# A shorter router, expert weights loaded further ahead, and a spread-out convolution in a two-block transformer kernel

## The reference, cut to what matters

```python
h = rmsnorm(x, norm1_g); proj = h @ w_in
ya = windowed_gqa(...)                      # 8 heads, window of 128
ym = mlstm_branch(qm, km, vm, om, gates...) # first: a depthwise convolution of 5 taps over q and k, then silu
u  = gates[:, :D] * (ya @ w_branch_attn) + gates[:, D:] * (ym @ w_branch_mlstm)
x  = x + u @ w_out
x  = x + hier_moe(rmsnorm(x, norm2_g))
# hier_moe: 4 groups of 8 experts; argmax group; top 2 experts in it, softmax weights
# each expert: (silu(t @ w_gate[e]) * (t @ w_up[e])) @ w_down[e], 1024 -> 512 -> 1024
```

## Time and profile before

| what | value |
|---|---|
| median of 3 runs | 2285.16 us (2284.2 to 2285.91) |
| the profiled execution: its time | 2284.88 us |
| the profiled execution: its span | 2283.0 us |
| mean granted clock of PE | 0.955 |
| PE busy | 2037.0 us, 89% of the span |
| DVE, ACT, POOL busy | 672.9, 590.4, 678.4 us |
| DMA traffic | 362.43 MB, of which the 192 expert loads are 201 MB |

### The profile page before, as it was taken

The page is one execution under the profiler, slowest core; times in us unless marked ns, Lnnn a source line. Parts: engine busy times, 40 slices in busy tenths (PEclk is TensorE's granted clock), DMA queues, the critical chain, the costliest instruction groups (busy, mean ns, idle before and its releaser), DMA issues.

```text
span 2283.0 us, 29374 instructions
## 1 busy us (share of the span) xinstructions
PE 2037.0 (89%) x10746; PEld 1446.5 (63%) x10747; DVE 672.9 (29%) x1145; ACT 590.4 (26%) x987; POOL 678.4 (30%) x383
## 2 busy tenths in 40 slices
PE   8987899999999999999999989997893887778884
PEld 7864688888888878888887756775782322222221
DVE  2348631110052243111007685124546000000002
ACT  2126333332212222333221325444420000000000
POOL 4421134444514434444451522222230000000000
PEclk9998999999999999999999989999896899999997
DMA  7311023332313324333231311210116899999996
GB/s 213 108 56 39 19 93 101 94 99 93 130 54 95 105 77 121 101 92 101 92 129 45 117 56 56 65 56 19 55 62 242 342 426 427 427 426 426 425 423 242
DMA packets 155405, 362.43 MB, mean 159 GB/s; under 512 B 16671, under 2 KB 88991, under 8 KB 130752
## 3 DMA queue, kind: packets, MB, share of 16 engines
q1 hardware_dynamic: 142880, 341.35, 40.5%
q10 hardware_dynamic: 7664, 11.64, 1.9%
q0 software_dynamic: 4784, 8.40, 1.0%
HBM read 355.58 MB, written 14.68 MB: 162 GB/s over the span
## 4 chain that ended last, share of the span: by engine, by line
PE 68%; DMA 16%; DVE 12%; issue 2%; ACT 1%; POOL 1%; SPq 0%; POOLq 0%; DVEq 0%; ACTq 0%
PE ps L1755 19%; PE ps L1757 18%; PE ps L1756 18%; DMA wpair<-l_expert 14%; PE ps L2239 5%; PE ps L2170 1%; DVE hres L1131 1%; DVE qkm L1406 1%; PE ps L2105 1%; DVE nmax L1209 1%; PE ps L2127 1%; POOL wlo L981 1%; DMA xg<-x2d,nowi 1%; DVE attn L1219 1%; PE ps L2151 1%
## 5 line engine op out<-in xcount | busy, mean ns | idle before, releaser
L981 POOL TENSOR_TENSOR wlo<-wraw,whi 128x1024 fp32r<-128x1024 f32 (+2 forms) x244 | 574.0, 2357 | 959.5 <-ACT whi L615 958.9
L1755 PE MATMUL ps<-xhi,whi 128*128 128x512 f32 (+2 forms) x1196 | 463.8, 388 | 3.2 <-ACT som L839 2.5
L1757 PE MATMUL ps<-xhi,wlo 128*128 128x512 f32 (+2 forms) x1196 | 460.5, 385 | 0.0
L1756 PE MATMUL ps<-xlo,whi 128*128 128x512 f32 (+2 forms) x1196 | 460.2, 385 | 0.0
L615 ACT CAST whi<-wraw 128x1024 fp32r<-128x1024 f32 (+2 forms) x244 | 245.9, 1014 | 608.0 <-PE ps L1757 581.4
L2239 PE MATMUL ps<-wpair,mx 128*32 128x512 f32 (+1 forms) x2048 | 249.9, 637 | 73.4 <-DMA wpair<-l_expert 72.1
L1755 PEld LDWEIGHTS ps<-xhi,whi 128*128 128x128 f32 x1196 | 226.2, 189 | 50.4 <-issue 7.5
L1757 PEld LDWEIGHTS ps<-xhi,wlo 128*128 128x128 f32 x1196 | 225.9, 189 | 44.1
L1756 PEld LDWEIGHTS ps<-xlo,whi 128*128 128x128 f32 x1196 | 226.2, 189 | 43.0
L2239 PEld LDWEIGHTS ps<-wpair,mx 128*32 128x32 f32 x2048 | 75.1, 116 | 247.2 <-issue 246.7
L1064 POOL COPY nowi<-idx 128x1 uint32 (+1 forms) x33 | 6.2, 187 | 479.5 <-DVE ybuf L1727 430.0
(11 more groups left out here) (403 smaller groups left out, 2370.7 us busy)
## 6 DMA issues: line engine op xcount, KB each, us to landing
wpair<-l_expert SPq DMA_DIRECT2D x192, 1024.0 KB, 25.4
wraw<-ffn_w_gate SPq DMA_DIRECT2D x88, 256.0 KB, 2.8
wraw<-ffn_w_up SPq DMA_DIRECT2D x88, 256.0 KB, 3.0
wraw<-ffn_w_down SPq DMA_DIRECT2D x44, 512.0 KB, 3.5
wraw<-w_in SPq DMA_DIRECT2D x36, 512.0 KB, 3.5
wraw<-attn_w_qkv SPq DMA_DIRECT2D x24, 512.0 KB, 9.1
wraw<-conv_w_in SPq DMA_DIRECT2D x96, 128.0 KB, 2.2
wraw<-attn_w_o SPq DMA_DIRECT2D x8, 512.0 KB, 3.5
```

The lines of the kernel that those rows point to most:

```text
L981: pool.tensor_tensor(l, wraw[:, s, :, 0:cols], h.bitcast(F32), ALU.subtract).then_inc(w_lo, 1)
L1755: pe.matmul(dst, ahi, bhi, start=start, stop=False)
L1756: pe.matmul(dst, ahi, blo, start=False, stop=False)
L1757: return pe.matmul(dst, alo, bhi, start=False, stop=stop)
```

## The change

It has three parts.

1. **Router.** The logits of the first three tiles are computed before the last tile has been turned, and copied by DVE (`keep_logits`) between the normalisation and the split of the last tile. The last tile's logits are then made with the tokens as the stationary operand, so they need no turning. The counting products and the one-hot products become fp32r (`counting`, `both`, `sel`, `blk1`). The DVE sequence is rewritten with fewer instructions; what only the later turns need (`be`, the number of turns) comes after `routed` and sets a new semaphore `units_ready`. POOL's first gather reads `idx` directly and no longer waits for the number of turns.
2. **Expert loads.** Six more slots `wextra` are used. Seven loads are issued once `u_lo` is 2, six once `w_out` is done, four once the logits are turned and one once the tokens are stored. That is 18 of the 192 before `units_ready`. Turn 1 has a fixed pair of experts too. Turns 1 and 2 use the extra slots in part; from turn 4 on, the ring is the old one of 12 slots.
3. **Attention stage.** The six instructions of each gate scan are done two at a time, in steps 0 to 5. The 40 taps are done two at a time, in steps 6 to 25. Silu is applied to four convolutions in step 18 and to four in step 27.

```diff
             def moe_loads(sp):
...
-                sp.wait_ge(w_used, pair[0])
-                load_experts(EXPERTS // 2, 0)
-                sp.wait_ge(routed, 1)
+                early = (EXPERTS // 2 + 1, 1)
+                sp.wait_ge(u_lo, 2)
+                for s in range(4, 10):
+                    load(wexp[s][:, :], s, EXPERTS // 2, 0, m_loaded[s])
+                load(wextra[5], 5, *early, m_extra[5])
+                sp.wait_ge(w_used, pair[0])
+                for s in (0, 1, 2, 3, 10, 11):
+                    load(wexp[s][:, :], s, EXPERTS // 2, 0, m_loaded[s])
+                sp.wait_ge(logits_turned, 1)
+                for s in range(4):
+                    load(wextra[s], s, *early, m_extra[s])
+                for n in range(2):
+                    sp.wait_ge(x2_stored[n], 32)
+                load(wextra[4], 4, *early, m_extra[4])
+                sp.wait_ge(units_ready, 1)
...
+                for s in range(6, SLOTS):
+                    sp.wait_ge(m_used, s - 6 + 1)
+                    load(wexp[s - 6][:, :], s, *early, m_loaded[s - 6])
+                ea, eb = expert(4), expert(5)
+                for s in range(SLOTS):
+                    if s < 6:
+                        sp.wait_ge(m_used, s + 6 + 1)
+                        load(wexp[s + 6][:, :], s, ea, eb, m_loaded[s + 6])
+                    else:
+                        sp.wait_ge(m_used, SLOTS + s - 6 + 1)
+                        load(wextra[s - 6], s, ea, eb, m_extra[s - 6])
+                ea, eb = expert(6), expert(7)
+                for s in range(SLOTS):
+                    sp.wait_ge(m_used, SLOTS + s + 6 + 1)
+                    load(wexp[s][:, :], s, ea, eb, m_loaded[s])
-                with sp.Fori(0, more) as i:
+                with sp.Fori(3, more) as i:
                     load_experts(expert(i * 2 + 2), expert(i * 2 + 3), i)
...
-                if 10 <= k < 14:
-                    for n in range(2 * (k - 10), 2 * (k - 10) + 2):
+                if k in (18, 27):
+                    for n in range(MH) if k == 18 else range(MH, 2 * MH):
                         act.wait_ge(conv_done, n + 1)
...
             def gather(n):
-                if not isinstance(n, int) or n > 0:
+                if isinstance(n, int) and n == 0:
+                    rows = idx[:, 0, 0:1]
+                else:
                     pool.wait_ge(xg_turned, n)
-                column(0, n)
+                    column(0, n)
+                    rows = nowi[:, 0, 0:1]
...
-                if k < 2:
-                    gate_scan(k)
-                elif k < 10:
-                    conv(k - 2)
+                if k < 6:
+                    gate_scan(k // 3, k % 3)
+                elif k < 6 + MH * TAPS:
+                    for n in range(2 * (k - 6), 2 * (k - 6) + 2):
+                        conv(n // TAPS, n % TAPS)
...
+            def keep_logits():
+                dve.wait_ge(logits_full, 1)
+                run(dve.tensor_copy(lgT[0:ROUTE, 0:3 * P], ps[0:ROUTE, 0, 0:3 * P]), Count(logits_kept))
+
+            norm_stage(DC, add_half, add_rest, tail=RING, aside=keep_logits)
...
+            run(dve.tensor_tensor(lgb[:, :, :], lg, tok4(rbias, ROUTE), ALU.add))
...
+            run(dve.tensor_copy(c_, ps[:, 3, 0:EXPERTS]))
+            run(dve.tensor_tensor(heavy[:, 0, :], c_[:, lo16], c_[:, hi16], ALU.is_ge))
+            run(dve.tensor_tensor(most, c_[:, lo16], c_[:, hi16], ALU.max))
...
+            run(dve.tensor_tensor(eboth[:, :, :, :], pick[:, :, :, :].rearrange("p k t e -> p (k t) e").unsqueeze(2).to_broadcast([P, n8, 2, EXPERTS]),
+                                  table[:, :, :].unsqueeze(1).to_broadcast([P, n8, 2, EXPERTS]), ALU.mult))
+            run(dve.tensor_reduce(rs[:, 12:14, :, :].rearrange("p m k t -> p (k t) m"), eboth[:, :, :, :], AX_X, ALU.add))
...
+            run(dve.tensor_copy(second[one, 0:hx], wider[one, :]))
+            dve.wait_ge(slots_full, 1)
+            run(dve.tensor_scalar(idx[:, :, 0:PAIRS], ps[:, 4, 0:2 * PAIRS].rearrange("p (m b) -> p m b", m=2), float(NOBODY), None, ALU.add), Count(routed))
...
             for k in range(DC):
-                mm = three(ps[0:ROUTE, 0, :], rwhi[:, k, :], rwlo[:, k, :], xhi[:, k, :], xlo[:, k, :], k == 0, k == DC - 1)
+                mm = three(ps[0:ROUTE, 0, three_tiles], rwhi[:, k, :], rwlo[:, k, :], xhi[:, k, three_tiles], xlo[:, k, three_tiles],
+                           k == 0, k == DC - 1)
             mm.then_inc(logits_full, 1)
+            turn_normed(3, normed)
             pe.wait_ge(logits_kept, 1)
+            for t in range(3):
+                pe.transpose(ps[:, 1, t * ROUTE:(t + 1) * ROUTE], lgT[0:ROUTE, t * P:(t + 1) * P], ident[0:ROUTE, 0:ROUTE])
+            for k in range(DC):
+                if k % 4 == 0:
+                    pe.wait_ge(xt_lo, xlow.now - 1 + k // 4)
+                mm = three(ps[:, 1, 3 * ROUTE:TILES * ROUTE], xhi[:, k, last_tile], xlo[:, k, last_tile], rwhi[:, k, :], rwlo[:, k, :],
+                           k == 0, k == DC - 1)
+            mm.then_inc(logits_turned, 1)
```

More of the change, by code:

```diff
@@ L435, in build @@
         m_used = sem("m_used")
+        m_extra = [sem(f"m_extra{n}") for n in range(6)]
         idx_now = sem("idx_now")
@@ L966, in _ @@
             keep_tokens(1)
+            act.wait_ge(units_ready, 1)
+            more = act.value_load(be[0:1, UNITS:UNITS + 1], min_val=EXPERTS // 2 - 1, max_val=PAIRS - 1)
             with act.Fori(0, more) as i:
@@ new lines, in _ @@
+            run(dve.tensor_tensor(home, home, mine, ALU.add))
+            run(dve.tensor_tensor(earg[:, 1:5, :].rearrange("p g t -> p t g"), gl, col(R(0), GROUPS2), ALU.subtract))
+            run(dve.tensor_tensor(earg[:, 0, :], R(4), R(2), ALU.subtract), Count(e_arg))
+            dve.wait_ge(ranks_full, 1)
+            cum, c_ = ps[:, 2, 0:TILES * EXPERTS], blkcnt[:, 2, :]
+            run(dve.tensor_copy(c_, ps[:, 3, 0:EXPERTS]))
+            most, least, fits, wider = (share[:, n, :] for n in range(4))
@@ new lines, in _ @@
+            for k in range(TOP):
+                run(dve.tensor_tensor(sel[:, k * TILES:(k + 1) * TILES, :], turned.unsqueeze(1).to_broadcast([P, TILES, P]),
+                                      rs[:, 8, k, :].unsqueeze(2).to_broadcast([P, TILES, P]), ALU.is_equal), sr)
+            one = slice(0, 1)
+            run(dve.tensor_copy(second[one, 0:hx], wider[one, :]))
+            dve.wait_ge(slots_full, 1)
+            run(dve.tensor_scalar(idx[:, :, 0:PAIRS], ps[:, 4, 0:2 * PAIRS].rearrange("p (m b) -> p m b", m=2), float(NOBODY), None, ALU.add), Count(routed))
@@ L1583, in _ @@
+            run(dve.tensor_reduce(bef[one, 0:MORE], befl, AX_X, ALU.add))
+            swapped = be[one, EXPERTS:UNITS].rearrange("p (n h) -> p h n", h=2)
+            units = bef[one, 0:MORE].rearrange("p (n h) -> p h n", h=2)
+            for h in range(2):
+                run(dve.tensor_scalar(swapped[:, 1 - h, :], units[:, h, :], float(EXPERTS - 1), None, ALU.min), step if h == 0 else Count(units_ready))
             dve.wait_ge(e_exp, 1)
@@ L1704, in _ @@
-            run(dve.memset(idx[:, :, PAIRS:PAIRS + 4], 4095))
-            run(dve.tensor_copy(idx[:, :, 0:PAIRS], slots[:, :, :]), Count(routed))
             more = dve.value_load(be[0:1, UNITS:UNITS + 1], min_val=EXPERTS // 2 - 1, max_val=PAIRS - 1)
@@ L2219, in _ @@
-            pe.matmul(ps[:, 3, 0:EXPERTS], ones, upto[:, 3, :], start=True, stop=True).then_inc(ranks_full, 1)
+            for t in range(TILES):
+                pe.matmul(ps[:, 2, t * EXPERTS:TILES * EXPERTS], ones if t else before, every[:, 0:(TILES - t) * EXPERTS],
+                          start=(t == 0), stop=(t == TILES - 1))
+            for t in range(TILES):
+                mm = pe.matmul(ps[:, 3, 0:EXPERTS], ones, both[:, t, :], start=(t == 0), stop=(t == TILES - 1))
+            mm.then_inc(ranks_full, 1)
```

359 lines of the change are left out of this document (170 added, 189 removed).

## The result

The changed kernel takes 2234.76 us (median of 4 runs, 2233.52 to 2236.04), the kernel before beside it 2285.53 (4 runs, 2284.2 to 2289.49): a ratio of 0.9775, 95% interval 0.9758 to 0.9792, or 51 us faster. In a second group of runs it took 2234.78 (5 runs, 2231.45 to 2239.23) and the kernel before beside it 2281.23 (17 runs, 2274.33 to 2287.88): a ratio of 0.9787 (0.9767 to 0.9808), or 46.5 us faster. The forecast was 2235.5 us, a gain of 49.7. The profiled execution has a span of 2232.0 us against 2283.0.

The account below looks back on a forecast made before the run. Experts were taken as bound by weight transfer (DMA 99% busy), the earlier stages by PE. Stage gains add: 19.5 + 16.4 + 14.8 - 1.0 = 49.7 us off 2285.2 gives 2235.5 us, range 2226 to 2250.

Parts of the forecast that it names:

- Attention, forecast 19.5 us: Attention steps 0 to 14: spreading DVE's side work removes PE's stalls and slow clock, gaining 19.5 us, at most 23.5.
- Router, forecast 16.4 us: Router up to the first gather: earlier logits and fewer instructions save 16.4 us in all, bounds 12 and 18.5.
- Step (a): Router, logits: early products for three tiles bring the first router instruction 5.2 us earlier, bounds 3 and 6.
- Step (b): Router, first router instruction to first instruction on the counts: 7.6 us instead of 8.76, saving 1.1.
- Step (c): Router, counts to `routed`: fewer instructions make it 12.7 us instead of 21.2, saving 8.5, bounds 7 and 9.5.
- Step (d): Router, `routed` to POOL's first gather: 0.2 us instead of 1.8, without the register load and copy.
- Loads, forecast 13.8 us: Expert stream: six fewer loads after its start save 14.8 us, less 1 us charged for a shallow queue.
- the third rival: Expert stream: the old ring gives the lead of six loads back, up to 14.8 us, ending at 2249.3; chance 0.07.
- the fourth: Expert loads after turn 3: DMA queue depth lost, 3.3 us latency per pair, slower than before, up to 2522 us; chance 0.03.
- A: Attention tap steps: the taps run into POOL's subtraction, 11 us less gain, ending at 2246.5; chance 0.12.
- B: Before the expert stream: early loads are late and the first gather takes 12.33 us, not 4.50, ending at 2243.3; chance 0.07.
- E: Attention stage: spreading changes nothing because the attention chain itself holds PE, ending at 2255; chance 0.05.

Follow-up runs that it names:

- no_spread: Changed kernel with the attention part undone (whole gate scans in steps 0 and 1, taps in steps 2 to 9, silu in 10 to 13): 2257.90 us.
- router_only: Changed kernel with the attention and the load parts undone, so the router part alone: 2268.59 us, ratio 0.9939 to the kernel before.
- old_loads: Changed kernel with the load part undone (twelve loads of turn 0, a ring of 12 in every turn): 2249.92 us.

## The experiments: what held PE in the attention stage

My prediction took the gain of this stage as a difference of two totals, and didn't say how much scans, taps and silu each had cost. The lengths of the steps, from one maximum's start to the next, show it in three places:

```
step            0     1     2     3      4     5     6      7     8      9     10    11    12    13    14
before         8.55  8.95  7.16  10.11  10.06  7.15  10.12  7.46  11.23  7.93  7.78  5.08  7.80  5.08  11.92
changed        5.04  6.47  4.52   7.25   8.43  4.56   7.24  7.46  10.44  6.30  7.78  5.08  7.80  5.08   7.80
before_silu    8.54  9.04  7.16  10.15  10.06  7.19   7.51  7.46  11.23  7.95  7.78  5.08  7.80  5.08   7.80
scan_whole     8.55  8.72  4.79   7.24   6.77  5.00   7.24  7.46  10.44  6.31  7.78  5.08  7.80  5.08   7.80
taps_4         5.05  6.47  4.53   7.24   8.44  4.59   7.24  7.63  11.23  7.93  7.78  7.36  9.60  7.37   9.62
```

**Step 14** had no work of DVE's beside it, yet it took 11.92 us. The timelines of ACT and PE of the kernel before say why:

```profile
1420.55 1.28 ACT L875 ACT_TABLE_LOAD   x1
1421.85 1.33 ACT L875 ACTIVATE qkm<-qkm,vecs 128x512 f32<-128x512 f32 x2
1423.20 1.28 ACT L839 ACT_TABLE_LOAD   x1
1424.49 2.07 ACT L839 ACTIVATE som<-ps 128x512 f32<-128x512 f32 x4
...
1425.23 0.47 PE L1755 MATMUL ps<-xhi,whi 128*128 128x512 f32 x1 [2.48 <-ACT som L839]
```

ACT made the last two silus of step 13, loaded another table for `som`, and PE waited 2.48 us for its banks. The products behind it then ran at the slow clock for about 3 us. The prediction let silu's move cost and give nothing.

**before_silu** moves silu alone: `if k in (18, 27)` in the kernel before, as in the last lines of the diff of no_spread read backwards.

> The kernel before with silu alone moved, from steps 10 to 13 to steps 18 and 27; gate scans and taps whole, as before. In the trace of before, step 14 lasted 11.92 us and in that of the changed kernel 7.80: ACT loaded its tables for silu, then for som, and PE waited 2.48 us for som and fell to the slow clock. Theory: that stall is silu's alone, so step 14 returns to 7.8 and the kernel ends 4 us sooner (2281, -2.5 to -5.5). Rival, as my prediction has it: silu's move is worth nothing, 2285.

Measured: step 14 takes 7.80 us, so the stall was silu's, and PE's waits for `som` are gone. The time is 2279.92 us (2276.26 to 2284.67, 12 runs) against 2281.23 (17 runs) in that group, ratio 0.9986 (0.9975 to 0.9997): a gain of 0.7 to 5.7 us, which holds the 4.1 of the trace but can't settle its size. (Step 6 is shorter by 2.6 us too in this trace, and in that of router_only step 3 by 2.6 and step 6 by 1.1, where the code is as before: the slow clock behind a wait again.)

**scan_whole** has the gate scans whole in steps 0 and 1, the rest as changed.

```diff
-                if k < 6:
-                    gate_scan(k // 3, k % 3)
-                elif k < 6 + MH * TAPS:
+                if k < 2:
+                    for third in range(3):
+                        gate_scan(k, third)
+                elif 6 <= k < 6 + MH * TAPS:
```

> The changed kernel with the two gate scans whole in steps 0 and 1, taps in steps 6 to 21 and silu as changed. Theory: steps 0 and 1 take 8.55 and 8.9 us as before instead of 5.05 and 6.47, steps 2 to 5 stay or lose a little: 6 us slower than the changed kernel (5 to 7), 2240.7. Rival (the taps alone held PE and a whole scan is hidden behind PE's work): 0 to 1 us.

Measured: 2238.60 us (2234.03 to 2241.25, 5 runs), 3.8 above the changed kernel (2234.8, in another group), and 4.8 in the trace's steps 0 to 14. Both are below my range of 5 to 7; the rival is refuted. Steps 0 and 1 lose 5.8 us as expected. But step 4 gets 1.7 back, since no scan stands ahead of its scaling then.

**taps_4** makes the taps of a whole convolution in each of the steps 6 to 13.

```diff
-                elif k < 6 + MH * TAPS:
-                    for n in range(2 * (k - 6), 2 * (k - 6) + 2):
-                        conv(n // TAPS, n % TAPS)
+                elif k < 6 + 2 * MH:
+                    for tap_no in range(TAPS):
+                        conv(k - 6, tap_no)
```

The texts on record speak of four taps a step (here and for no_spread) and of the changed kernel's taps in steps 6 to 21 (here and for scan_whole). Both are slips of mine: a convolution has five taps (one instruction of 0.49 us and four of 0.75), this kernel makes all five in a step as the kernel before does, and the changed kernel makes two a step up to step 25.

> The changed kernel with four taps a step in steps 6 to 13 instead of two in steps 6 to 21; gate scans and silu as changed. Theory (chain of DVE in a step, maximum 0.8, taps 3.1, scaling 0.8, plus 2.1 when one of them meets POOL's subtraction, against 4.4 us in a one-half step): steps 11 and 13 take about 7.2 instead of 5.1, and of the two-half steps those behind them up to 10.1: 12 us slower than the changed kernel (9 to 16), 2247. Rival (each step's taps fit but for the one-half steps): 4 to 5 us. Rival (the lock alone, exposed once in each of the eight steps): 17 us. I look for which instruction meets the subtraction.

Measured: 2244.66 us (2242.88 to 2249.39, 5 runs), 9.9 above the changed kernel, inside the theory's bounds and not near either rival. Steps 0 to 14 are 10.8 us longer, and 1.1 comes back later, since steps 20 to 23 have no taps. (With five taps the chain is 5.2 us even without a clash, over the 4.4 of a one-half step.) The timelines of DVE, POOL and PE in step 11 of this kernel show the whole mechanism:

```profile
1386.91 5.10 DVE L1449 SCALAR_TENSOR_TENSOR qkm<-cpad,vecs,qkm 128x512 f32<-128x512 f32 x4
...
1388.30 2.38 POOL L1016 TENSOR_TENSOR wlo<-wraw,whi 128x1024 fp32r<-128x1024 f32 x1 [5.38 <-ACT whi L651]
...
1392.91 0.55 PE L2134 MATMUL ps<-ident,scr 128*128 128x128 f32 x3 [2.43 <-DVE scr L1490]
...
1394.90 0.63 PE L1774 MATMUL ps<-whi,xlo 128*128 128x512 f32 x1
1395.33 0.63 PE L1772 MATMUL ps<-whi,xhi 128*128 128x512 f32 x1
```

The four longer taps take 5.10 us instead of 3.11, for one of them stands while POOL subtracts. The scaling comes late, PE waits 2.43 us, and its products then have the slow clock (0.43 us apart instead of 0.23). In seven of the eight steps the taps were hit in this way. A two-half step hides it if PE is at the full clock (step 10: 7.78); a one-half step does not (11, 13), and the clock carries the loss into the next one (12, 14).

In the changed kernel all 32 of these taps take 0.75 us and none is hit. What the subtraction meets there is the scaling that follows, or the addition ahead of it:

```profile
1368.78 1.54 DVE L1449 SCALAR_TENSOR_TENSOR qkm<-cpad,vecs,qkm 128x512 f32<-128x512 f32 x2
...
1370.69 2.40 POOL L1016 TENSOR_TENSOR wlo<-wraw,whi 128x1024 fp32r<-128x1024 f32 x1 [7.98 <-ACT whi L651]
...
1370.75 2.56 DVE L1490 TENSOR_SCALAR scr<-scr,rsum 128x384 f32<-128x384 f32 x1
```

It takes 2.56 us instead of 0.42. This happens in 11 of the 32 steps, and in none of the kernel before: the addition is stopped in steps 1 and 4 (2.17 and 2.22 us instead of 0.16), the scaling in 7, 9, 10, 15, 17, 20, 22, 24 and 25. In a two-half step it is done before PE asks. Of the others PE waited 1.2 us in step 4 and 0.46 us each in steps 20 and 22, and steps 20 to 23 are 1.1 us longer than before. By the rule of the Trainium skill that the prediction weighed (SBUF — State Buffer, "SBUF: two separate sides") the trace agrees: the scaling lasts 2.14 us longer beside a subtraction of 2.40.

## The experiments: the gather and the clock

**late_loads** makes the second rival, early loads that run into the first gather, come true.

```diff
-                sp.wait_ge(u_lo, 2)
-                for s in range(4, 10):
-                    load(wexp[s][:, :], s, EXPERTS // 2, 0, m_loaded[s])
-                load(wextra[5], 5, *early, m_extra[5])
                 sp.wait_ge(w_used, pair[0])
-                for s in (0, 1, 2, 3, 10, 11):
+                for s in range(SLOTS):
                     load(wexp[s][:, :], s, EXPERTS // 2, 0, m_loaded[s])
+                load(wextra[5], 5, *early, m_extra[5])
```

> The changed kernel with its seven early loads moved behind the last use of the old weights, with the others of turn 0; all else as changed. Eighteen loads then run from 1696.5, at 2.75 us each until about 1746, and the first gather, issued at 1729.5, runs among them: 10 to 12 us instead of 4.6. Theory: the first expert product is 6.5 us later and with it the end, 2241 (2239 to 2244). Rival (the transfers were idle before the stream anyway, and their work is only moved): no difference, 2234 to 2236. Rival (slots of turn 0 themselves late): more than 9 us.

Measured: 2238.92 us (2235.39 to 2246.85, 5 runs), 4.1 above the changed kernel beside it (2234.78) and at the lower edge of the range that I gave, 2239 to 2244. The chain that ended last, and the stretch up to the end of these loads:

```profile
1727.45 8.45 DMA xg<-x2d,idx
```

```profile
1696.50:1743.00 46.50, 18.30 (x98) 13.38 (x100) 23.52 (x90) 5.17 (x7) 3.25 (x5) 0.57 1.01 419
```

DMA is full until 1743, as expected, and the first expert product comes 3.8 us later after `idx` (12.9 against 9.0). The stream doesn't make up for it. So the rival's mechanism is real and wasn't at work in the changed kernel. Its price was put too high: a gather among loads took 8.45 us here, not the 12.33 of the earlier trace rows, nor the 10 to 12 of my expectation.

**warm** and **warm_gather**. The router's part fell short of my sum. In the changed kernel the granted clock is 0.50 (1.2 GHz) from 1705 to 1740, and the last logit products show the moment, 0.11 us apart and then 0.21:

```profile
1704.63 0.26 PE L1774 MATMUL ps<-rwhi,xlo 128*128 128x36 f32 x1
1704.74 0.27 PE L1772 MATMUL ps<-rwhi,xhi 128*128 128x36 f32 x1
1704.85 0.38 PE L1773 MATMUL ps<-rwlo,xhi 128*128 128x36 f32 x1
1705.07 0.38 PE L1774 MATMUL ps<-rwhi,xlo 128*128 128x36 f32 x1
```

All that PE does afterwards in the router is short and lies on the path. These two kernels put products of no use into its waits.

```diff
+            def keep_busy(times):
+                for _ in range(times):
+                    pe.matmul(ps[:, 7, 0:2 * P], before, counting[:, :, :].rearrange("p a n -> p (a n)"), start=True, stop=True)
+
+            keep_busy(24)
             pe.wait_ge(picked, 1)
...
             mm.then_inc(ranks_full, 1)
+            keep_busy(44)
...
             mm.then_inc(slots_full, 1)
+            keep_busy(26)
```

> The changed kernel with products of no use (256 columns, to a bank that nobody reads) in three waits of PE in the router: 24 behind the last logits, 44 behind the counts, 26 behind the one-hot products while the first gather runs. In the changed kernel the granted clock is 0.50 from 1705 to 1740, so PE's own steps there run at 1.2 GHz: counting products 2.0 us, one-hot products 1.9, turning the tokens 1.94, and 3.4 us for the first sixteen expert products. Theory (the router and gather came out 2 us short of my sum by this clock): the granted clock stays near 1.00 and the stream starts 3 us sooner against the first maximum of step 31 (1 to 4.5), end at 2231.8. Rival (the clock doesn't rise, or what PE does there is hidden): 0. Rival (the added products delay PE's own): later by 1 to 3 us.

> The same with the third group alone, 26 products behind the one-hot products. Theory: turning the tokens and the first expert products at the full clock, 1 to 2 us sooner, 2233.3. Rival (26 products after 10 us of idleness don't raise the clock in time): 0.

Measured: 2229.79 us (2227.35 to 2230.46, 5 runs) for all three groups and 2231.71 (2230.59 to 2232.38, 5 runs) for the third alone, on another chip than after_again; beside the kernel before (2283.57, 9 runs) 0.9768 (0.9748 to 0.9787) and 0.9779 (0.9759 to 0.9798). By medians that is 5.0 and 3.1 us under the changed kernel. The intervals of the ratios overlap with that of the changed kernel, so the traces have to bear this out, and they do. Busy times of warm by stretch, and its chain that ended last:

```profile
1725.00:1730.00 5.00, 5.00 (x24) 5.00 (x24) 3.48 (x13) 0.00 (x0) 1.08 (x1) 0.50 0.34 131
1730.00:1735.00 5.00, 3.39 (x24) 2.99 (x27) 0.95 (x6) 1.23 (x2) 0.97 (x3) 0.83 0.22 63
1735.00:1740.00 5.00, 5.00 (x48) 1.55 (x52) 0.00 (x0) 1.07 (x1) 0.43 (x1) 1.00 0.36 83
```

```profile
1728.08 4.44 DMA xg<-x2d,idx
...
1732.66 1.08 PE ps L2316 x8
```

Turning the gathered tokens takes 1.08 us instead of 1.96. The first expert products start at 1.00, so the first slots fall free sooner: SP's next load starts 3.7 us behind the first product instead of 6.2. The stream as the table counts it lasts 456.5 us instead of 459.1. The third group gives both (0.9 us from `idx` to the first product, 2.8 in the stream), more than the 1 to 2 us that I expected of it. The other two are worth the shorter counting products (1.1 us for the eight instead of 1.9); the rest of their 2 us in the column of the stage behind can't be told from that column's own spread. The one-hot products still had the slow clock, and my expectation that it would stay near 1.00 was wrong: it was 0.50 again from 1705 to 1710 and from 1725 to 1730. Nor is the slow clock what my sum had missed, as that expectation says, for the kernel before had it too: 0.53 from 1751 to 1780, with the turning at 1.98 us. The parts that the sum did miss are named below.

**after_again** is the changed kernel once more.

> The changed kernel, unchanged, so that the others of this group have it beside them: 2234.8 (2231 to 2238). Steps 0 to 14 again close to 102.7 us; the stage behind the attention may start up to 2 us sooner or later against it by the granted clock of its first products.

Measured: as the table shows, the same to 0.02 us in the median, although the profiled execution's span is 2237.4 us, 5.4 above the first.

## Why the prediction came out right

**Attention, forecast 19.5 us.** Steps 0 to 14 gained 25.1 us, steps 15 to 31 gave 1.1 back, and the stage behind 2.8. I had not seen the last: between the first and the last diagonal of that stage the same 166 products took 55.9 us at a granted clock of 0.82, where they had taken 53.1 at 0.87 (busy times by stretch of the changed kernel, and then of the kernel before):

```profile
1531.10:1587.00 55.90, 43.46 (x166) 27.52 (x165) 26.29 (x55) 26.40 (x82) 13.31 (x10) 0.82 0.09 29
```

```profile
1555.70:1608.80 53.10, 40.72 (x166) 26.37 (x164) 26.28 (x54) 26.37 (x83) 13.35 (x10) 0.87 0.09 30
```

From step 31 to `idx` the profiles with the spreading have 1.4 to 3.9 us more than those without it and with the same router, the two with added products aside. Why the slow phases fall otherwise there stays open. The net, 21.2 us in the traces and 19.2 to 23.1 by the medians, is close to the forecast partly by luck: my figure for the ideal stage (107.1 us at most) was 4.5 us above the 102.6 that it reached (127.7 less 25.1), and steps 20 to 23 and the clock behind the stage took 3.9 us back. And 1.6 us of the 25.1 hang on the clock in step 5 of the one execution that was profiled. My list of causes was incomplete too, as step 14 shows; it entered the sum only because I worked from the total of the stage. That silu costs nothing in its new place was right: steps 18 and 27 are 7.80 and 7.25 us long, and the 1.1 us of steps 20 to 23 are there in every trace with two taps a step and not in taps_4, which has no taps there.

**Router, forecast 16.4 us.** Step (a): the first router instruction came at 1730.0 on the old time scale, forecast 1729.4; 4.6 us instead of 5.2. Step (b): 7.60 us to the counts, as forecast. Step (c): 12.8 us from the counts to `routed`, forecast 12.7. So adding up small DVE instructions at about 0.20 us each, from rows of their own shapes, was good to 0.1 us over the 41 instructions of this step. Step (d) failed: the gather was issued 0.93 us after `routed` instead of 0.2. Of this 0.81 us is "issue", time in which POOL waits for nothing that the profile shows. The 1.82 us of before held a register load, a copy and another small instruction, with never more than 0.20 us of "issue" at a time between them, so the sum took the removed pieces for the whole; what POOL does in the 0.81 us no run shows. Then the first slots fell free 0.5 us later behind the first product than before. In all 14.3 us by the trace (36.15 us for the start of the stream, less the 21.87), and 13.9 by router_only.

**Loads, forecast 13.8 us.** Measured 15.2 by old_loads. The term of 14.8 us was right (14.6 in the stream). The 1 us charged for the shallow queue at turns 3 and 4 was not there: DMA keeps 99% over the whole stream, and 1.00 to 1.03 in every 5 us from 1815 to 1860. That ended the third rival and the fourth.

**The rivals.** A, the taps meet POOL's subtraction, did not come about with two taps a step: the order within a step, on which the prediction built, held for the taps. But that argument left out the scaling right behind them. In nine of the twenty tap steps it was stopped in their place, so DVE's chain was the 5.3 us of the rival there and not the 3.2 of the forecast. That it cost 1.1 us and not 11 is because only two of the nine are one-half steps (20 and 22), and that is luck. taps_4 shows that the clash is real and costs 10 us with five. B was refuted in the changed kernel and made in late_loads, at 4.1 us instead of 7.8. E is refuted by the 103.5 us.

## What to carry to other kernels

Divide the length of each step by what its engine must do before asking what held it: three different causes (scans, taps, and an unrelated function table on ACT) stood in one total here, and only the table of steps parted them. Work that shares an engine with a critical chain is best put where its end comes before another engine's clash with it begins; two taps in a step cost about 1 us in all, five in a step 10 us more. What follows the moved work on its engine has to be checked for the same clash. And where one core's PE waits in a serial stage, look at the granted clock of the next steps on the path: 26 products of no use, put into a wait that is a transfer's, brought 3 us.

## What the runs showed of the hardware that was not expected

- POOL's subtraction of two tensors from SBUF also stops DVE instructions that I had not thought of: a scaling of one tensor by a column (0.42 us, and 2.56 with it), an addition of two columns of 128 x 1 (0.16, and 2.17), a negation of 4 rows (0.42, and 2.38 in scan_whole).
- A gather of 128 rows took 4.3 to 4.6 us with DMA little used, 8.45 us among the loads of late_loads, and 12.33 in the full stream of the kernel before.
- Single executions of one kernel are up to 13.6 us apart (before: 2274.33 to 2287.88 in 17 runs). The first maximum of the attention stage alone comes 9 us apart, in identical code: a single profile says little of a few us in the span, but much in the difference of two landmarks.
